# Two token tiles interleaved word by word in the stationary buffers, and the buffers moved within 256 bytes

## What is computed

```python
h = h + 0.5 * swiglu(rmsnorm(h, g_ffn1), w_ffn1_in, w_ffn1_out)      # hidden width 5632
z = rmsnorm(h, g_mix) @ w_mix_in                                     # 2048 -> 5 x 1024
y_conv = gate_b * causal_dwconv(gate_c * h_c)                        # 1024 channels
y_gm   = u * (tril(w_spatial) @ norm(v) + b)                         # 8 heads x 128
h = h + concat(y_conv, y_gm) @ w_mix_out
h = h + xattn(rmsnorm(h, g_xattn), rmsnorm(mem, g_mem), w_xq, w_xk, w_xv, w_xo)
h = h + 0.5 * swiglu(rmsnorm(h, g_ffn2), w_ffn2_in, w_ffn2_out)
out = rmsnorm(h, g_final)
```

## Time and profile before

| | before |
|---|---|
| median of 3 executions | 2189.3 us (2188.56 to 2189.32) |
| profiled execution, first to last instruction | 2187.2 us |
| TensorE matmul busy | 2167.1 us, 99% |
| VectorE busy | 1349.3 us, 62% |
| ScalarE busy | 991.6 us, 45% |
| read from HBM | 409.01 MB, 188 GB/s over the span |

### The profile page before, as it was taken

The page is one execution under the profiler, slowest core; times in us unless marked ns, Lnnn a source line. Parts: engine busy times, 40 slices in busy tenths (PEclk is TensorE's granted clock), DMA queues, the critical chain, the costliest instruction groups (busy, mean ns, idle before and its releaser), DMA issues.

```text
span 2187.2 us, 25558 instructions
## 1 busy us (share of the span) xinstructions
PE 2167.1 (99%) x9626; PEld 1778.9 (81%) x9626; DVE 1349.3 (62%) x1549; ACT 991.6 (45%) x1103; POOL 1.8 (0%) x7
## 2 busy tenths in 40 slices
PE   8999999999999999999999999999999999999998
PEld 6888888888888888888888888888888888888886
DVE  5676667666474547865677554576676667664544
ACT  5444454444343444444554444454444444443433
POOL 0000000000000000000000000000000000000000
PEclk9999999999999999999999999999999999999999
DMA  6666666665556565665556445466666666665553
GB/s 227 209 190 197 195 191 188 197 195 189 188 171 204 181 191 181 195 227 175 180 170 207 155 159 169 157 212 197 193 191 193 192 192 190 195 194 187 188 188 135
DMA packets 159217, 412.20 MB, mean 188 GB/s; under 512 B 12588, under 2 KB 13732, under 8 KB 158756
## 3 DMA queue, kind: packets, MB, share of 16 engines
q1 hardware_dynamic: 157728, 410.04, 60.2%
q10 hardware_dynamic: 1412, 1.11, 0.2%
HBM read 409.01 MB, written 2.10 MB: 188 GB/s over the span
## 4 chain that ended last, share of the span: by engine, by line
PE 96%; DVE 2%; ACT 1%; DMA 0%; issue 0%; ACTq 0%; DVEq 0%
PE ps L906 94%; PE ps L935 1%; DVE w_lo L575 1%; PE ps L919 1%; DVE ps L635 1%; DVE convT L748 0%; DVE xT_lo L583 0%; DMA h<-in_x 0%; ACT convT L444 0%; PE ps L1023 0%; ACT xT_hi L329 0%; ACT w_hi L321 0%; DVE stage L738 0%; ACT scratch L555 0%; ACT zT L441 0%
## 5 line engine op out<-in xcount | busy, mean ns | idle before, releaser
L575 DVE TENSOR_TENSOR w_lo<-raw,w_hi 128x1024 fp32r<-128x1024 f32 x768 | 936.1, 1224 | 773.8 <-ACT w_hi L321 768.6
L321 ACT ACTIVATE w_hi<-raw 128x1024 fp32r<-128x1024 f32 x768 | 811.8, 1061 | 1106.0 <-PE ps L906 1087.0
L906 PE MATMUL ps<-w_hi,xT_hi 128*128 128x512 f32 x1856 | 573.8, 390 | 5.3 <-DVE w_lo L575 5.3
L906 PE MATMUL ps<-w_lo,xT_hi 128*128 128x512 f32 x1856 | 572.2, 389 | 0.0
L906 PE MATMUL ps<-w_hi,xT_lo 128*128 128x512 f32 x1856 | 572.0, 389 | 0.0
L906 PEld LDWEIGHTS ps<-w_hi,xT_hi 128*128 128x128 f32 x1856 | 347.8, 188 | 78.9 <-issue 4.1
L906 PEld LDWEIGHTS ps<-w_lo,xT_hi 128*128 128x128 f32 x1856 | 349.0, 188 | 72.7
L906 PEld LDWEIGHTS ps<-w_hi,xT_lo 128*128 128x128 f32 x1856 | 348.7, 188 | 72.8
L906 PE MATMUL ps<-w_hi,hidT_hi 128*128 128x512 f32 x704 | 223.5, 397 | 0.4 <-DVE w_lo L575 0.4
L906 PE MATMUL ps<-w_hi,hidT_lo 128*128 128x512 f32 x704 | 222.7, 395 | 0.0
L906 PE MATMUL ps<-w_lo,hidT_hi 128*128 128x512 f32 x704 | 221.3, 393 | 0.0
(11 more groups left out here) (119 smaller groups left out, 800.7 us busy)
## 6 DMA issues: line engine op xcount, KB each, us to landing
raw<-in_w_ffn_in SPq DMA_DIRECT2D x352, 512.0 KB, 4.1
raw<-in_w_ffn_out SPq DMA_DIRECT2D x176, 512.0 KB, 4.3
raw<-in_w_mix_in SPq DMA_DIRECT2D x80, 512.0 KB, 4.2
raw<-in_w_mix_out SPq DMA_DIRECT2D x32, 512.0 KB, 3.7
raw<-in_w_xq SPq DMA_DIRECT2D x32, 512.0 KB, 3.8
raw<-in_w_xk SPq DMA_DIRECT2D x32, 512.0 KB, 3.9
raw<-in_w_xv SPq DMA_DIRECT2D x32, 512.0 KB, 3.6
raw<-in_w_xo SPq DMA_DIRECT2D x32, 512.0 KB, 3.6
```

The source lines that it names most:

```text
L321: nc.scalar.activation(w_hi[:, k % RING, :], raw[:, k % RAW, :], ACT.Copy).then_inc(hi_ready, 1)
L575: nc.vector.tensor_tensor(w_lo[:, k % RING, :], raw[:, k % RAW, :], w_hi[:, k % RING, :].bitcast(F32), ALU.subtract).then_inc(lo_ready, 1)
L906: ins = nc.tensor.matmul(bank(s, t * GW + b * BLK, BLK), xs[:, k, t * P:(t + 1) * P], ws_[:, k % RING, b * BLK:(b + 1) * BLK], start=(k == ...
```

## The change

Each stationary activation buffer gets the shape unit, position in tile, tile: the words of the two tiles alternate. A row still has 1024 bytes, but the stationary operand of one tile is now 128 words, each 8 bytes from the next, over all of them; tile 1 starts 4 bytes behind tile 0. The functions that write these buffers write with the same step. `kT`, which is a moving operand, keeps adjacent words and is now a tensor of its own over the memory of `xT`. New padding puts `xT` and the weight slots at 0 modulo 256, and `hidT`, `yT`, `memT` at 64 modulo 256: the moving operand lies 0 bytes ahead of the stationary one for `xT`, as before, and 192 ahead (before: 96) for the other buffers. `pT`, `v_hi`, `v_lo` keep their shape; both move by multiples of 32 bytes. No engine gets an instruction more or fewer, and the order is the same.

```diff
+    PITCH = 256
+    def lane(at, to):
+        return at + (to - at) % PITCH
...
-    xT_hi = put("xT_hi", [P, KD, SEQ], F32R)
-    xT_lo = put("xT_lo", [P, KD, SEQ], F32R)
+    at_x = lane(place["at"], 0)
+    place["at"] = at_x + 32 * KB
+    xT_hi = put("xT_hi", [P, KD, P, TOK], F32R, at=at_x)
+    xT_lo = put("xT_lo", [P, KD, P, TOK], F32R, at=at_x + 16 * KB)
+    kT_hi = put("kT_hi", [P, KD, SEQ], F32R, at=at_x)
+    kT_lo = put("kT_lo", [P, KD, SEQ], F32R, at=at_x + 16 * KB)
+    place["at"] = lane(place["at"], 0)
...
-    big = extra + 8 * KB
-    hidT_hi = put("hidT_hi", [P, KF, SEQ], F32R, at=big)
+    big = lane(extra + 8 * KB, 64)
+    hidT_hi = put("hidT_hi", [P, KF, P, TOK], F32R, at=big)
...
+        def by_tile(T, k):
+            return T[:, k, :, :].rearrange("p b t -> p t b")
+        def pair_by_tile(T, k):
+            return T[:, bass.ds(k, 2), :, :].rearrange("p k b t -> p k t b")
...
-                        ins = nc.scalar.activation(dst[:, k0 + k, :], bank(s, k * SEQ, SEQ), ACT.Copy, scale=col(g, k0 + k))
+                        ins = nc.scalar.activation(by_tile(dst, k0 + k), bank(s, k * SEQ, SEQ).rearrange("p (t b) -> p t b", t=TOK),
+                                                   ACT.Copy, scale=col(g, k0 + k))
...
+            def lo_tiled(dst, hi, k0, s, banks, first):
+                for b in range(banks):
+                    dve.wait_ge(hi_taken, first + b + 1)
+                    nc.vector.tensor_tensor(pair_by_tile(dst, k0 + 2 * b),
+                                            bank(s, b * BLK, BLK).rearrange("p (k t b) -> p k t b", k=2, t=TOK),
+                                            pair_by_tile(hi, k0 + 2 * b).bitcast(F32), ALU.subtract).then_inc(taken, 1)
...
-                                ins = nc.tensor.matmul(bank(s, t * GW + b * BLK, BLK), xs[:, k, t * P:(t + 1) * P],
+                                ins = nc.tensor.matmul(bank(s, t * GW + b * BLK, BLK), xs[:, k, :, t],
```

More of the change, by code:

```diff
@@ L142, in build @@
     g_fin = put("g_fin", [P, D], F32, at=extra)
-    big = extra + 8 * KB
-    hidT_hi = put("hidT_hi", [P, KF, SEQ], F32R, at=big)
[L145 to L149, removed]
+    big = lane(extra + 8 * KB, 64)
+    hidT_hi = put("hidT_hi", [P, KF, P, TOK], F32R, at=big)
+    hidT_lo = put("hidT_lo", [P, KF, P, TOK], F32R, at=big + KF * KB)
+    yT_hi = put("yT_hi", [P, KD, P, TOK], F32R, at=big)
+    yT_lo = put("yT_lo", [P, KD, P, TOK], F32R, at=big + 16 * KB)
+    memT_hi = put("memT_hi", [P, KD, P, TOK], F32R, at=big + 32 * KB)
+    memT_lo = put("memT_lo", [P, KD, P, TOK], F32R, at=big + 48 * KB)
     c_buf = put("c_buf", [P, TOK, GW], F32, at=big + 32 * KB)
@@ L337, in hi_plain, with hi_tiled @@
                                          bank(s, (b0 + b) * BLK, BLK), ACT.Copy).then_inc(hi_taken, 1)
+            def hi_tiled(dst, k0, s, banks, ready, first):
+                for b in range(banks):
+                    act.wait_ge(ready, first + b + 1)
+                    nc.scalar.activation(pair_by_tile(dst, k0 + 2 * b),
+                                         bank(s, b * BLK, BLK).rearrange("p (k t b) -> p k t b", k=2, t=TOK),
+                                         ACT.Copy).then_inc(hi_taken, 1)
             def squares(src, c, name):
@@ L373, in ffn_in @@
                         hi_units(unit0, 4, 11)
[L374 removed]
+                        hi_tiled(hidT_hi, i * 8 + 4 * j, j, 2, turned, i * 4 + (TURN[f"ffn{f}_in0"] + 2 * j))
                         hi_units(unit0, 11, KD)
@@ L382, in ffn_out @@
                 hi_units(u0, 4, 11)
-                hi_plain(hidT_hi, 4 * (FG - 1), SET[last], 2, turned, TURN[last])
+                hi_tiled(hidT_hi, 4 * (FG - 1), SET[last], 2, turned, TURN[last])
                 hi_units(u0, 11, KF)
@@ L450, in _ @@
             act.wait_ge(yc_product, 1)
-            nc.scalar.activation(yT_hi[:, 0:HALF, :], convT[:, :, :], ACT.Copy).then_inc(yc_hi, 1)
+            nc.scalar.activation(yT_hi[:, 0:HALF, :, :].rearrange("p k b t -> p k t b"),
+                                 convT[:, :, :].rearrange("p k (t b) -> p k t b", t=TOK), ACT.Copy).then_inc(yc_hi, 1)
             hi_units(u, LATE + 1, KD)
@@ L475, in _ @@
             hi_units(u, 0, 8)
-            hi_plain(yT_hi, HALF, SET["U"], 4, turned, TURN["U"])
+            hi_tiled(yT_hi, HALF, SET["U"], 4, turned, TURN["U"])
             hi_units(u, 8, KD)
@@ L497, in _ @@
             root("mem", TOK)
-            hi_plain(qT_hi, 0, SET["q0"], 4, turned, TURN["q0"])
+            hi_tiled(qT_hi, 0, SET["q0"], 4, turned, TURN["q0"])
             hi_units(u, LATE, KD)
@@ L502, in _ @@
             hi_units(u, 0, LATE)
-            hi_plain(qT_hi, HALF, SET["q1"], 4, turned, TURN["q1"])
+            hi_tiled(qT_hi, HALF, SET["q1"], 4, turned, TURN["q1"])
             hi_units(u, LATE, KD)
@@ L530, in _ @@
                 hi_units(u, 4, 9)
-                hi_plain(yT_hi, pair * HALF, s, 4, pv_done, 4 * pair)
+                hi_tiled(yT_hi, pair * HALF, s, 4, pv_done, 4 * pair)
                 hi_units(u, 9, KD)
@@ L582, in lo_scaled @@
                         k = 2 * b + j
-                        ins = nc.vector.scalar_tensor_tensor(out=dst[:, k0 + k, :], in0=bank(s, k * SEQ, SEQ),
-                                                             scalar=col(g, k0 + k), in1=hi[:, k0 + k, :].bitcast(F32),
+                        ins = nc.vector.scalar_tensor_tensor(out=by_tile(dst, k0 + k),
+                                                             in0=bank(s, k * SEQ, SEQ).rearrange("p (t b) -> p t b", t=TOK),
+                                                             scalar=col(g, k0 + k), in1=by_tile(hi, k0 + k).bitcast(F32),
                                                              op0=ALU.mult, op1=ALU.subtract)
@@ L669, in ffn_in @@
                         lo_units(unit0, 9, 11)
-                        lo_plain(hidT_lo, hidT_hi, i * 8 + 4 * j, j, 2, i * 4 + (HI[f"ffn{f}_in0"] + 2 * j))
+                        lo_tiled(hidT_lo, hidT_hi, i * 8 + 4 * j, j, 2, i * 4 + (HI[f"ffn{f}_in0"] + 2 * j))
                         lo_units(unit0, 11, KD)
@@ L683, in ffn_out @@
                 lo_units(u0, 9, 11)
-                lo_plain(hidT_lo, hidT_hi, 4 * (FG - 1), SET[last], 2, HI[last])
+                lo_tiled(hidT_lo, hidT_hi, 4 * (FG - 1), SET[last], 2, HI[last])
                 lo_units(u0, 11, KF)
@@ L760, in _ @@
             dve.wait_ge(yc_hi, 1)
-            nc.vector.tensor_tensor(yT_lo[:, 0:HALF, :], convT[:, :, :], yT_hi[:, 0:HALF, :].bitcast(F32),
+            nc.vector.tensor_tensor(yT_lo[:, 0:HALF, :, :].rearrange("p k b t -> p k t b"),
+                                    convT[:, :, :].rearrange("p k (t b) -> p k t b", t=TOK),
+                                    yT_hi[:, 0:HALF, :, :].rearrange("p k b t -> p k t b").bitcast(F32),
                                     ALU.subtract).then_inc(yc_ready, 1)
@@ L785, in _ @@
             lo_units(u, 4, 8)
-            lo_plain(yT_lo, yT_hi, HALF, SET["U"], 4, HI["U"])
+            lo_tiled(yT_lo, yT_hi, HALF, SET["U"], 4, HI["U"])
             lo_units(u, 8, KD)
@@ L811, in _ @@
                     norm("mem", halves, D, rstd_mem[:, :])
-                lo_plain(qT_lo, qT_hi, c * HALF, SET[f"q{c}"], 4, HI[f"q{c}"])
+                lo_tiled(qT_lo, qT_hi, c * HALF, SET[f"q{c}"], 4, HI[f"q{c}"])
                 lo_units(u, LATE, KD)
@@ L845, in _ @@
                 lo_units(u, 4, 9)
-                lo_plain(yT_lo, yT_hi, pair * HALF, s, 4, HI[f"pv{pair}"])
+                lo_tiled(yT_lo, yT_hi, pair * HALF, s, 4, HI[f"pv{pair}"])
                 lo_units(u, 9, KD)
```

4 lines of the change are left out of this document (1 added, 3 removed).

## The result

The changed kernel takes **2213.7 us** (median of 4), before 2189.1: a ratio of 1.0112, 95% interval 1.0097 to 1.0126. It is 24.6 us slower, where 2087 us was forecast.

What follows compares the result with a forecast made beforehand. TensorE's distance from one matmul to the next was taken to bound the kernel. 2189.3 - 104.3 (9216 matmuls at 218 ns) + 2 (V group) = 2087 us; range 2062 to 2193, likeliest case 2066 to 2105.

Steps and rivals of the forecast that it cites:

- What bounds the kernel: TensorE, busy 2167.1 of 2187.2 us: the distance between matmul starts, 226.7 ns for 5568 and 233.3 for 3648.
- the step of the stationary operand: In weight loads: doubled, it advances twice as fast in bytes, nearer the moving operand's pace; 218 ns a matmul in all groups.
- The term of 104 us: All 9216 matmuls at 218 ns make 2009.1 us, a gain of 104.3 us; by the bounds 122.7 and 85.9.
- the gate's 216 ns: Distance of the gate's 16 plain float32 matmuls, taken as the lower bound of the new distance.
- That the loss comes once with each weight load: Unit matmuls: one meeting is left to each load, so at most 220 ns, halfway between 213.3 and 226.7.
- Placement: `xT` keeps distance 0, the others go from 96 to 192: at most 24 us, contained in the main gain.
- only the placement counts: Rival for the unit matmuls: the step changes nothing, 192 is as good as 0; 2165 us. Placement or partial effects: 0.19.
- More memory touched: Slow case for the weight loads, which cover 1024 bytes instead of 512; chance 0.20.
- Writing the buffers: ScalarE and VectorE write and read with a step of 8 bytes; a possible excess at hand-overs was taken as 0.
- The V group: VectorE, busy 50.5 of 60 us there, gets tight with units of 2.62 us instead of 2.72; 2 us added.
- The lower bound, 2066: Whole kernel: total in us if every unit matmul reaches 216 ns; low end of the likeliest case, chance 0.50.
- Attention: 96 scores have an interleaved stationary operand: at most 96 x 13 ns = 1.2 us gained, counted as 0.

Runs made afterwards that it cites:

- 6: Adjacent words, fewer stationary words or only 384 or 256 columns per matmul, against padded kernels with adjacent words: 2210.3, 2199.4, 1806.8 and 1729.1 us.
- step_four: Kernel before, but the stationary operand of the unit matmuls takes every fourth word over two rows, 2048 bytes: 2242.9 us.
- adjacent_new_places: Changed kernel's places (moving operand 0 and 192 bytes ahead), but words adjacent as in the kernel before: 2188.0 us, ratio 0.9995.
- adjacent_all_zero: Kernel before with padding only: words adjacent, every stationary buffer and weight slot at 0 modulo 256, distance 0 everywhere: 2166.1 us, ratio 0.9893.
- experiment 2: Weight slots padded so that several distances occur in one kernel, with adjacent, alternating and again adjacent words: 2208.7, 2216.6 and 2204.2 us.
- 5: Five kernels with constant distances, only the places of `xT` and the other buffers moved, words adjacent or alternating: 2223.6, 2198.4, 2217.2, 2217.7 and 2224.8 us.
- few_columns: Adjacent words at distance 0 everywhere, but hi by lo uses 64 and lo by hi 32 of 128 stationary words, save in a group's last unit: 2210.3 us.
- short_load: Adjacent words at distances 0 and 192, but hi by lo uses 32 of 128 stationary words, save in a group's last unit: 2199.4 us.

## Why the prediction was wrong

- **What bounds the kernel** was right: TensorE's distance from start to start, in two families by address, was all that moved, and the sum over both gives the measured change (24.8 us).
- **The step that failed** is the step of the stationary operand. The forecast assumed that a matmul loses time where the reading of the two operands meets in memory, and that two which advance at one pace meet all the time or never; so the loss was to fall to one meeting a load, 220 ns or less. No row and no run shows such meetings. The paces became equal or nearly so (9.1 to 9.6 bytes a ns, by the estimate in 6), but at all eight distances modulo 256 in steps of 32 the matmul keeps 230.0 to 233.3 ns. The two families did come apart, but neither came near 220. Nor are there meetings to be counted over a load: at distance 0 a quarter of the load leaves the loss where it was, and a stationary operand of one word, which doesn't advance at all, still loses 18 ns. The term of 104 us had no row behind it. Of its bounds, 220 ns starts from 213.3 ns for 512 columns, which no run took: 215.8 ns was the least, with a moving operand of one word, and 213.3 is what the 0.417 ns a column give. The other, the gate's 216 ns, belongs to 256 columns, a moving operand at half the pace (0.84 ns a column); the trace before could not tell whether a slow moving operand or an equal pace makes the gate cheap. The forecast took the second; that it came first among the cases was judgement, not evidence.
- **What the runs showed in its place**: the loss needs a moving operand that walks through memory (215.8 ns without; the gate's pass of 256 columns, whose moving operand walks at half the pace, takes 216). It depends on distance and step together: a loss of 13.3, 16.7 or 20.0 ns for 512 columns where a rhythm has settled (226.7, 230.0, 233.3 ns), a mean in between (229, 231, 232 ns) where none of these did, and up to 23.4 ns in `step_four` (236.7 ns). Adjacent words at distance 0 are the best combination found. The change gave it up for 5568 matmuls, 6.6 ns each, and bought 3.3 ns for most of the other 3648.
- **That the loss comes once with each weight load** was right in form at distance 0 and wrong as a cause: 13.3 ns at 256, 384 and 512 columns are a price for each matmul, but halving or quartering the load beside it changes less than 1 ns, and at another distance, 192, 256 columns lose only 6.7 ns. The rows before did not show it: the scores of the earlier trace rows lie 96 bytes apart, and at 96 a matmul of 512 columns loses 20 ns, one of 256 columns 13.
- **Placement**: that distance matters by itself and is worth up to 24 us was right in size, but for 0, not for 192: `adjacent_new_places` won nothing and `adjacent_all_zero` 22.8 us. The rival "only the placement counts", 2165 us, described a kernel that the change was not.
- **More memory touched** had the sign right and the cause wrong: at distance 0 four times the memory costs 10 ns (236.7 against 226.7), at 96 nothing (233.3), and at distance 0 one word costs more than 128 (231 against 226.7).
- **Writing the buffers**: no cost, as said; VectorE at 476 and 682 ns. **The V group** was given 2 us for a faster TensorE. TensorE became slower, so that term was not tried. The lower bound, 2066, leaves these 2 us out; with them it is 2069.
- **Attention**: the 13 ns that the forecast allows each score are 120.0 less 106.7 ns, again by the 0.417 ns a column. The 96 scores stay at 120.0 ns on the mean, so this loss did not go either; with adjacent words and the same distance of 192 (`adjacent_new_places`) they take 113.5.
- **Chances**: 0.22 for slower was too little. The trace had one sign that a good place could be lost: `xT` was already the cheaper family, and the change kept its distance while altering its step. The forecast counted a gain for both.

What stays open: why distance and step act as they do. The values of a settled rhythm lie 3.3 ns apart on the mean (226.7, 230.0, 233.3), eight times the 0.417 ns of a column; a new one needs several matmuls to settle (experiment 2), and an interruption can exchange one for another (5). No run shows what sets these values. No kernel was run without weight loads between its matmuls, nor with an fp32r moving operand that walks at half the pace; so it isn't shown whether the loss needs a load at all. And a product with fewer stationary words takes more time, about 235 ns a matmul in `few_columns` and 231 in `short_load`, for a reason that no run shows.

## What to carry to other kernels

When one shape of matmul shows two distances from start to start in a full-rate stretch, compare the addresses of its operands before anything else: here a few bytes of padding were worth 1.1% of the whole kernel. Take the better family as the target and change one thing, not layout and place together; and measure the combination, since distance, step and number of columns don't add up. Take the mean over whole groups, because the same operands can run in more than one rhythm. A gain that rests on a mechanism without a row deserves less than the even chances that it got here, above all where the cheap case might be an accident that the change removes.

## What the runs showed of the hardware

- A matmul of fp32r with 512 columns took 215.8 ns with a moving operand of one word, and 226.7 to 233.3 (up to 236.7 with a stationary step of four words) with one that walks through memory, by the places of the two operands modulo 256 and the stationary operand's step. At distance 0 a column more took 0.417 ns (512, 384, 256 columns: 226.7, 173.3, 120.0 ns). At some distances the same operands ran at 230.0 or at 233.3, and an interruption by sixteen transposes switched between them.
- A weight load's record is 0.83 ns a word (between 32 and 128 words) on top of some 80; 188 ns for 128 adjacent words, 195 with a step of two words, 308 to 314 with four. The matmul beside it doesn't take the difference: 233.3 ns beside each of the three, 96 bytes ahead.
- The distance between starts was a repeating pattern (231, 232, 237 ns before, with `hidT`, 700 ns together); its mean, 233.3 ns, is what a timeline over 12 matmuls gives.
- VectorE wrote and read words 8 bytes apart in the same 476 and 682 ns as adjacent ones; ScalarE took 499 instead of 484 ns for 256 and 624 instead of 584 for 512.
